# Two-block transformer in one kernel: matmul pairs of two PSUM banks taken apart, and the norm callbacks of three items moved by one unit

## What is computed

```python
# first block
h = rmsnorm(x, g_mix);  z = h @ w_in
cb, cc, cv, q, k, v, f_logit, gate_c, gate_a = split(z)
conv_branch = (cb * causal_dwconv(cc * cv, conv_w)) @ w_conv_out
attn_branch = forgetting_attention(q, k, v, log_sigmoid(f_logit + b_f)) @ w_attn_out
merged = sigmoid(gate_c + b) * conv_branch + sigmoid(gate_a + b) * attn_branch
x = x + merged @ w_mix_out
x = x + square(relu(rmsnorm(x, g_mlp) @ w_ff1)) @ w_ff2      # 2048 -> 8192 -> 2048
x = rmsnorm(x, g_final)
# second block
q, k, v, p = split(rms_norm(x, attn_norm_g) @ w_in_2)         # q, k normed per head
x = x + concat([moba_attention(q, k, v, rel_bias), multiscale_pool(p)]) @ w_out_2
x = x + conv_ffn(rms_norm(x, ffn_norm_g))                     # w_up_2, width-3 conv, silu(gate)*val, w_down_2
```

## Time and profile before

| | |
|---|---|
| median of 3 runs | 2424.62 us (2423.96 to 2424.97) |
| the profiled execution | 2423.96 us, span 2422.2 us |
| TensorE matmul busy | 2401.4 us, 99% |
| VectorE, ScalarE busy | 63%, 48% |
| DMA | 450.58 MB, mean 186 GB/s |

### The profile page before, as it was taken

The page is one execution under the profiler, slowest core; times in us unless marked ns, Lnnn a source line. Parts: engine busy times, 40 slices in busy tenths (PEclk is TensorE's granted clock), DMA queues, the critical chain, the costliest instruction groups (busy, mean ns, idle before and its releaser), DMA issues.

```text
span 2422.2 us, 30337 instructions
## 1 busy us (share of the span) xinstructions
PE 2401.4 (99%) x12645; PEld 2051.0 (85%) x12645; DVE 1515.3 (63%) x1534; ACT 1169.4 (48%) x1360; POOL 0.2 (0%) x4
## 2 busy tenths in 40 slices
PE   8999999999999999999999999999999999999999
PEld 6788888888888888888888888888888888888887
DVE  5465566666566566566466666855777577756774
ACT  5454445545544344344344555554555455535552
POOL 0000000000000000000000000000000000000000
PEclk9999999999999999999999999999999999999999
DMA  7556556565555565555565555555656665666664
GB/s 231 174 156 192 157 190 187 188 191 190 186 180 191 192 217 190 192 182 200 192 190 175 200 171 168 166 174 175 191 175 207 191 187 178 202 194 185 184 207 142
DMA packets 236902, 450.58 MB, mean 186 GB/s; under 512 B 16449, under 2 KB 19643, under 8 KB 236635
## 3 DMA queue, kind: packets, MB, share of 16 engines
q1 hardware_dynamic: 235995, 447.49, 58.2%
q10 hardware_dynamic: 768, 1.14, 0.1%
HBM read 446.46 MB, written 2.11 MB: 185 GB/s over the span
## 4 chain that ended last, share of the span: by engine, by line
PE 96%; DVE 3%; ACT 1%; DMA 0%; issue 0%; SPq 0%; DVEq 0%; ACTq 0%
PE PS L69 96%; DVE WL L69 1%; ACT WH L69 0%; DVE TA L69 0%; DMA RAW<-in_w_in 0%; DVE TC L69 0%; DVE XHL L69 0%; DVE XT L69 0%; DVE TB L69 0%; ACT TA L69 0%; DVE PB L69 0%; SPq L69 0%; DVE NC L69 0%; ACT SQ L69 0%; DVE RB L69 0%
## 5 line engine op out<-in xcount | busy, mean ns | idle before, releaser
L69 DVE TENSOR_TENSOR WL<-RAW,WH 128x1024 fp32r<-128x1024 f32 (+1 forms) x844 | 1022.2, 1220 | 760.1 <-ACT WH L69 759.8
L69 ACT ACTIVATE WH<-RAW 128x1024 fp32r<-128x1024 f32 (+1 forms) x845 | 881.9, 1054 | 921.2 <-PE PS L69 904.7
L69 PE MATMUL PS<-XHL,WH 128*128 128x512 f32 x3984 | 1253.4, 396 | 8.6 <-DVE XHL L69 6.4
L69 PEld LDWEIGHTS PS<-XHL,WL 128*128 128x128 f32 x3968 | 746.0, 188 | 176.3
L69 PE MATMUL PS<-XHL,WL 128*128 128x256 f32 x3968 | 780.1, 278 | 0.0
L69 PE MATMUL PS<-WH,MHL 128*128 128x512 f32 x2240 | 694.5, 390 | 1.1 <-DVE TA L69 1.1
L69 PEld LDWEIGHTS PS<-XHL,WH 128*128 128x128 f32 x3984 | 607.2, 188 | 13.5 <-DVE XHL L69 6.6
L69 PEld LDWEIGHTS PS<-WH,MHL 128*128 128x128 f32 x2240 | 420.5, 188 | 88.4 <-DVE TA L69 1.5
L69 PE MATMUL PS<-WL,MHL 128*128 128x512 f32 x1120 | 435.8, 389 | 0.0
L69 PEld LDWEIGHTS PS<-WL,MHL 128*128 128x128 f32 x1120 | 210.3, 188 | 42.8
L69 DVE TENSOR_TENSOR TA<-TA,PS 128x1024 f32<-128x1024 f32 x72 | 87.9, 1221 | 7.9 <-ACT TA L69 0.5
(11 more groups left out here) (126 smaller groups left out, 789.3 us busy)
## 6 DMA issues: line engine op xcount, KB each, us to landing
RAW<-in_w_ff SPq DMA_DIRECT2D x256, 512.0 KB, 3.7
RAW<-in_w_in SPq DMA_DIRECT2D x224, 512.0 KB, 3.8
RAW<-in_w_up SPq DMA_DIRECT2D x176, 512.0 KB, 3.8
RAW<-in_w_down SPq DMA_DIRECT2D x88, 512.0 KB, 4.2
RAW<-in_w_mix_out SPq DMA_DIRECT2D x32, 512.0 KB, 4.1
RAW<-in_w_out SPq DMA_DIRECT2D x32, 512.0 KB, 3.8
RAW<-in_w_conv_out SPq DMA_DIRECT2D x16, 512.0 KB, 3.5
RAW<-in_w_attn_out SPq DMA_DIRECT2D x16, 512.0 KB, 4.3
```

What stands on the lines that cost most here:

```text
L69: ins = step[1](*step[2], **step[3])
```

## The change

In `feature_item` the loop over pairs of banks (two H matmuls, then two L matmuls) becomes a loop over banks (one H, one L). In three items the callback of the norm moves from after unit 3 to after unit 4, and that of the spread from after unit 7 to after unit 6.

```diff
-                    for j0 in range(0, len(banks), 2):
-                        two = list(enumerate(banks))[j0:j0 + 2]
-                        for j, bank in two:
-                            PE.do(mm, PS[:, b + bank, :], h[:, k, j * P:(j + 1) * P], src[:, kc, :],
-                                  start=st, stop=False, inc=False)
-                        for j, bank in two:
-                            end = j == len(banks) - 1 and k == len(kcs) - 1
-                            t = PE.do(mm, PS[:, b + bank, 0:T], l[:, k, j * P:(j + 1) * P], src[:, kc, 0:T],
-                                      start=False, stop=en, inc=end)
+                    for j, bank in enumerate(banks):
+                        PE.do(mm, PS[:, b + bank, :], h[:, k, j * P:(j + 1) * P], src[:, kc, :],
+                              start=st, stop=False, inc=False)
+                        end = j == len(banks) - 1 and k == len(kcs) - 1
+                        t = PE.do(mm, PS[:, b + bank, 0:T], l[:, k, j * P:(j + 1) * P], src[:, kc, 0:T],
+                                  start=False, stop=en, inc=end)
...
-                mid = {2: [lambda: turn_x_item(3, G_MLP, xtok)], 3: [lambda: norm_columns("r2", "sum")],
-                       7: [lambda: spread_item("r2")]} if seg == 0 and g == 0 else {}
+                mid = {2: [lambda: turn_x_item(3, G_MLP, xtok)], 4: [lambda: norm_columns("r2", "sum")],
+                       6: [lambda: spread_item("r2")]} if seg == 0 and g == 0 else {}
...
-        it = w2_item(0, {2: [lambda: turn_x_item(3, G_AT2, nxt)], 3: [norm2_columns], 7: [lambda: spread_item("r3")]})
+        it = w2_item(0, {2: [lambda: turn_x_item(3, G_AT2, nxt)], 4: [norm2_columns], 6: [lambda: spread_item("r3")]})
...
-                mid = {2: [lambda: turn_x_item(3, G_FF2, xtok)], 3: [lambda: norm_columns("r4", "sum")],
-                       7: [lambda: spread_item("r4")]} if g == 0 else {}
+                mid = {2: [lambda: turn_x_item(3, G_FF2, xtok)], 4: [lambda: norm_columns("r4", "sum")],
+                       6: [lambda: spread_item("r4")]} if g == 0 else {}
```

More of the change, by code:

```diff
@@ L332, in feature_item @@
                     PE.wait([need(kc, tok)])
-                    st = first and k == 0
-                    en = last and k == len(kcs) - 1
-                    for j0 in range(0, len(banks), 2):
-                        two = list(enumerate(banks))[j0:j0 + 2]
-                        for j, bank in two:
-                            PE.do(mm, PS[:, b + bank, :], h[:, k, j * P:(j + 1) * P], src[:, kc, :],
-                                  start=st, stop=False, inc=False)
-                        for j, bank in two:
-                            end = j == len(banks) - 1 and k == len(kcs) - 1
-                            t = PE.do(mm, PS[:, b + bank, 0:T], l[:, k, j * P:(j + 1) * P], src[:, kc, 0:T],
-                                      start=False, stop=en, inc=end)
+                    for j, bank in enumerate(banks):
+                        st = first and k == 0
+                        en = last and k == len(kcs) - 1
+                        PE.do(mm, PS[:, b + bank, :], h[:, k, j * P:(j + 1) * P], src[:, kc, :],
[3 more added lines that the diff above has]
+                                  start=False, stop=en, inc=end)
                 hl_free[u] = t
```

## The result

| | before | after |
|---|---|---|
| median | 2424.8 us | 2445.3 us (2444.16 to 2447.24, 4 runs) |
| ratio | | 1.0084, 95% interval 1.0072 to 1.0095 |
| profiled execution, its span | 2423.96, 2422.2 | 2443.27, 2441.5 |

The account below looks back on a forecast made before the run. TensorE, busy 99% of 2422.2 us, was taken as the bound. Reordering 0 plus callbacks 0.65 + 0.65 + 1.4 gave +2.7 on the profiled 2423.96, and 0.66 for the median: 2427.3 us, range 2422.5 to 2433.8.

Parts of the forecast that it names:

- The reordering: Loop of H and L matmuls, H0 H1 L0 L1 to H0 L0 H1 L1: 0 us, ends -5.3 and +6.5 us.
- Rival A: Reordered loop: changes of width between H and L cost something, up to 6.5 us, 2433.8; chance 0.28.
- rival C: Reordered loop: a change of bank costs, so halving these saves 21 us, 2406; chance 0.07.
- The cover of the loads: Reordered loop: a weight load behind a single L (0.110 against 0.116 us) is hidden by 6 ns, before as after.
- The same bank (B): Reordered loop: an L must wait for its own bank's H; 42 us, 2469; chance 0.05. The forecast itself said no cost.
- The callbacks: Norm queued one unit later, spread issued one earlier, in three items: waits for DG outweigh saved RB waits, +2.7 us.
- r2 and r4: Two of the three spreads with moved callbacks: a new 1.3 us wait for DG, net +0.65 us each.
- r3: The spread with the longer norm chain: a 3.1 us wait for DG, net +1.4 us, at the bound +2.0.
- rival E: TensorE's clock falls to half in the wait at r3, costing 1.4 us more, 2428.7; chance 0.05.
- D: Moved callbacks don't stall, the norm's chain being ready; 0.65 us comes off three times, 2422.7; chance 0.08.

Follow-up runs that it names:

- e6: Kernel before, order H H L L, with L streaming all 512 columns instead of 256 in all chunks: 2868.1 us.
- e7: Changed order H L H L, callbacks as before, with L streaming all 512 columns instead of 256 in all chunks: 2867.5 us.
- e10: Changed order, callbacks as before, with L streaming 128 columns instead of 256 (all chunks but an item's first and last): 2398.3 us.
- e12: Kernel before, order H H L L, with H and L both loading 64 columns of weights instead of 128 (not an item's first and last chunks): 2430.9 us.
- e14: Changed order, callbacks as before, with H and L both loading 16 columns of weights instead of 128 (not first and last chunks): 2430.4 us.
- e3: Kernel before with order H0 H1 H2 H3 L0 L1 L2 L3, callbacks as before: 2434.97 us, ratio 1.0042.
- e5: Kernel before with order H0 H1 L1 L0, so each first L follows the H of its own bank: 2424.99 us, ratio 0.9998.
- e2_callbacks_only: Kernel before with only the callbacks moved, order of matmuls unchanged: 2428.85 us, ratio 1.0014.
- e13: Kernel before, order H H L L, with H loading 64 columns of weights instead of 128 (not an item's first and last chunks): 2419.3 us.
- e4: Kernel before with order H0 H1 L0 H2 L1 H3 L2 L3, callbacks as before: 2444.8 us, ratio 1.0083.

## Why the prediction was wrong

**The reordering, 0 with ends at -5.3 and +6.5: the step that failed.** It was put at nothing and cost 17.2. The failing step is "I take 0 for the reordering, the value of which f_item is the nearest row": it took f_item's 0.2321 for the pace of 512 columns on XHL, and so found a rest of 0.3 +/- 2.8 ns a group for everything else. e6 and e7 stream the same tile at 0.2267, the figure that the token items had shown. With it the columns of a group take 680 ns, and 697 - 680 = 17 ns were there before the change. Rival A, worked from that row, would have been priced at up to another 17 ns a group, 2112 x 17 = 36 us, and the range would have held the result. The mechanism would still have been wrong: what the runs show is no price for each change of width but two paces that the new order can fall into, at 346.7 and 353.3 ns a pair, where the old one has 348.3. The rows for that were before me; I weighed the 5 ns between them only as a price of bank changes (rival C), set it aside, and used the row that made the rest vanish.

**The cover of the loads, "hidden by 6 ns".** The six matmuls of the earlier trace rows gave 0.110 us, and e10's pair reads as a load that ends within 0.113. An L's 256 columns take 0.113, not the 0.116 that I counted, so the margin is about nothing. That nearness looks like what the states live on, since all is well where L is 512 wide; but e12 and e14 show that shorter loads don't cure it, so this stays a guess.

**The changes of width (rival A)** was right in direction and wrong as a count: e3 has the fewest and costs 9.8. **The same bank (B)** costs nothing, as predicted: e5, and e7 against e6. **The changes of bank (C)**: in the all-512 kernels the order alters their number and not the time; nothing there either.

**The callbacks, +2.7:** measured +3.7 in the median; in the trace 3.6 lie at the three places. r2 and r4 cost 0.4 each, not 0.65; the waits for DG there were 0.98, not 1.3 (in e2_callbacks_only they sum to 5.0 with the 3.04 of r3). r3 cost 2.8: 1.4 as worked out, and the clock for the rest. The rows had shown a stand-still that led to the half level, and rival E had its price right; its chance of 0.05 was too low for a wait that I put at 3.1 us myself. **D**, no stall, fell.

**What is shown and what isn't.** Shown: the order makes the loss; it does so through a pace that takes one of two steady values, doesn't follow what the other engines do, is flipped by a chunk in another order, and is single with 512-column L, and with 64-column H weights in the order H L H L (in H H L L these gave two paces, e13). Not shown: what in TensorE makes the two values. Why e3 runs at 350.8 ns a pair and e4 at 353.3 is open too. Theories W, S, G and the uncovered load each met a run that they can't explain.

## What to carry to other kernels

Take a floor for a matmul's pace from the fastest row with the same number of columns, not from the row that looks most alike; the rest above it is what a change of order can make larger or smaller. Where streams of different lengths alternate and the short one lasts about as long as a load of weights (here 256 columns and 128), the order is worth measuring even if it moves no work: H H L L ran at one pace everywhere, H L H L at two. And a callback moved to save 0.65 us of waiting must be checked for the chain behind it: at r3 the wait that it opened also took the clock down.

## What the runs showed that I had not expected

- One instruction sequence, same operands, same clock: 346.7 or 353.3 ns a pair, each held for up to hundreds of microseconds, and the slow one a cycle of three pairs, 350, 350 and 361 ns. Whether a disturbing chunk ends it hung on where in the cycle it came.
- Fewer columns to stream can be free of gain: 128 instead of 256 columns of L took 7 to 13 ns off a pair instead of 57; and less to load can cost: 64-column weights for both gave +5 us.
- A wait of 3.0 us in the middle of the kernel brought TensorE to 1.2 GHz, and the work behind it took 1.4 us more than at the full level; waits of 0.98 us didn't. The Trainium skill ("TensorE: Matmul & The Clock Gate", "Why this matters for your kernels") warns of such gaps between bursts; by that rule the trace agrees, with 0.93 granted in the window of the wait and 0.56 in the one behind it.
